# Loading the first two tiles and the input weights in another order, in an eight-core encoder step

## The chip, the cores and the metric

The kernel runs on one Trainium2 chip, on all 8 of its cores, with no traffic between them. Each core has its own engines: TensorE (PE), VectorE (DVE), ScalarE (ACT), GpSimd (POOL), SyncE (SP), and 16 DMA engines that all of a core's transfers share. The metric is the device time of the slowest core in microseconds; lower is better.

## The reference

One layer of an encoder trunk over 16384 prompt tokens and 8 x 32 sample tokens, width 1024. What matters here is its first half:

```
h  = RMSNorm(x)
z  = h @ W_in                      # 2048 columns, [B | C | v | u]
a  = B * causal_dwconv3(C * v)     # 512 channels
b  = scale * blockdiag_linear(trailing_mean(u) - u)   # windows 2, 4, 8, 16
x  = x + concat(a, b) @ W_out
x  = x + relu(RMSNorm(x) @ W_up)^2 @ W_down
x  = x + (p @ W_ple) * sigmoid(RMSNorm(x) @ W_ple_gate)
```

and a final RMSNorm. The last rows of C*v and of u are returned as states.

## The kernel before

Each core takes 2048 prompt tokens and 32 sample tokens, as NT = 5 tiles of 416 columns; x is held transposed, channels on the partitions, as 8 blocks k of 128 channels. Tile 0 has 16 columns of halo more (432). All of x stays in SBUF: X[0] to X[4]. Weights are cast from f32 in DRAM to bf16 by the transfers that POOL issues; x (f32) comes by transfers that SP or ACT issue.

W_in comes in eight pieces, win 0 to win 7 (`loadwin`, L782), each for two groups of 128 columns, in the order of `ZORDER`: u0 u1 | u2 u3 | v0 v1 | c0 c1 | b0 b1 | v2 v3 | c2 c3 | b2 b3. Tile t above 0 comes in two halves of four blocks (`loadx`, L786). The names used below:

- H(t): the tile times its gain in bf16, eight ACT instructions (`Norm.xg`, L472; the first stage does not multiply by 1/rms until PSUM is read).
- `Norm.pre`: squares of x (L493 on DVE, L494 on ACT) and their sum over blocks (L501, L510).
- S(t): the sum over partitions, a matmul with ones in f32 (L564), then the root on ACT (L547) and four reciprocals on DVE (L551), which everything that reads z from PSUM waits for: u (L633), v (L657), c (L662), b (L676).
- For u, POOL or DVE form the trailing sums (L641), DVE the difference (L646). For c, ACT (L665) and DVE (L668) form the convolution, and DVE or POOL scale it (L672).
- PE: z groups L608, block-diagonal matmuls L683, W_out groups L696. The first W_out group waits for everything of tile 0. After it come W_up (L722) and W_down (L734) for most of the time.

PE's program order is the order in which the code is written: the 16 matmuls of u0 and u1 of tile 0 (those of u0 each wait for their own block of H), S(0), then u2 to v1 of tile 0, then u0 to u3 of tile 1, S(1), and then the rest of tile 0 from c0 on. On ACT, DVE and POOL the order comes from a list scheduler (`Prog.schedule`), which simulates the program with assumed costs and a simple model of the transfers, and so gives another order when transfers move. Every engine then runs its list in order: an instruction that waits holds up all behind it. A transfer is issued by its engine in that order too, and `after` names transfers that must have landed first.

Before the change, SP issues blocks 0-1 and 4-5 of tile 0, ACT blocks 2-3 and 6-7. POOL issues win 0 at once; win 1 after blocks 0-1, win 2 after blocks 4-5, and the later ones each two or three transfers on. Tile 1 is issued once win 0 has landed, tile 2 once the first half of W_out has.

Of the kernel before, what the change touches and what calls it, by code (L numbers as in the profile page):

```python
# [12 lines left out]
KD = 8  # L13
# [6 lines left out]
TW0 = TN + NHALO  # L20
# [277 lines left out]
def build_program(debug=False):  # L298
    nc = bass.Bass("TRN2", target_bir_lowering=False)

    def din(name, shape):
        return nc.dram_tensor(name, list(shape), F32, kind="ExternalInput").ap()
# [4 lines left out]
    xt0 = din("xt0", (128, KD * TW0)); xt = din("xt", (NT - 1, 128, KD * TN))  # L307
# [13 lines left out]
    pg = Prog(nc)  # L321
# [4 lines left out]
    def vbf(off, n):  # L326
        return arena[:, off // 4: off // 4 + n // 2].bitcast(BF16)
# [13 lines left out]
    X = []  # L341
# [28 lines left out]
    wout = vbf(wout_o, 8192).rearrange("p (h k n) -> p h k n", h=2, k=KD)  # L370
# [410 lines left out]
    def loadwin(h, after=()):  # L781
        return pg.dma("pool", lambda e: e.dma_start(out=win[:, h, :, :], in_=w_in[h].rearrange("p (k n) -> p k n", k=KD)), 1024,  # L782
                      writes=[("win", h)], after=after)

    def loadx(t, after):
        return [pg.dma("sp", lambda e, hf=hf: e.dma_start(out=X[t][:, 4 * hf:4 * hf + 4, :],  # L786
                                                          in_=xt[t - 1][:, 4 * hf * TN:(4 * hf + 4) * TN].rearrange("p (k n) -> p k n", k=4)),
                       4 * TN / 2.0, writes=[("x", t, 4 * hf + i) for i in range(4)], after=after) for hf in range(2)]

    pg.dma("act", lambda e: e.dma_start(out=cst, in_=cstd), 90, writes=[("cst",)])  # L790
    wq = [loadwin(0)]
    xq = []
    for q4, eng in ((0, "sp"), (1, "act"), (2, "sp"), (3, "act")):
        xq.append(pg.dma(eng, lambda e, q4=q4: e.dma_start(out=X[0][:, 2 * q4:2 * q4 + 2, :],
                                                           in_=xt0[:, 2 * q4 * TW0:(2 * q4 + 2) * TW0].rearrange("p (k n) -> p k n", k=2)),
                         TW0, writes=[("x", 0, 2 * q4), ("x", 0, 2 * q4 + 1)]))
    pg.op("dve", lambda e: e.memset(epsb, EPS), 0.1, writes=[("epsb",)])
    pg.op("dve", lambda e: e.memset(ones, 1.0), 0.1, writes=[("ones",)])
    pg.op("act", lambda e: e.activation(out=RT[3][:, 0:1], in_=epsb[:, 0:1], func=AF.Sqrt), 0.2, reads=[("epsb",)],
          writes=[("rt", 3)], table="sqrt")  # L800
    wq.append(loadwin(1, [xq[0]]))
    wq.append(loadwin(2, [xq[2]]))
    pg.dma("pool", lambda e: e.dma_start(out=wpl, in_=w_pool.rearrange("p (g n) -> p g n", g=4)), 128, writes=[("wpl",)])
    x1 = loadx(1, [wq[0]])
    wq.append(loadwin(3, [wq[1]]))
    wq.append(loadwin(4, [wq[2]]))
    wq.append(loadwin(5, [x1[1]]))
    wq.append(loadwin(6, [wq[4]]))
    wq.append(loadwin(7, [wq[5]]))
    wo = [pg.dma("pool", lambda e, h=h: e.dma_start(out=wout[:, h, :, :], in_=w_out[h].rearrange("p (k n) -> p k n", k=KD)), 2048,  # L810
                 writes=[("wout", h)], after=[wq[6 + h]]) for h in range(2)]
    loadx(4, loadx(3, loadx(2, [wo[0]])))


    pg.op("dve", lambda e: e.tensor_copy(out=CS.hcv[:, :, 0:2], in_=sthist[:, :, 0:2]), 0.1, reads=[("cst",)],
          writes=[("hcv", "s", c) for c in range(4)])
    pg.op("dve", lambda e: e.tensor_copy(out=CS.U[:, :, 0:15], in_=sthist[:, :, 2:17]), 0.1, reads=[("cst",)],
          writes=[("U", "s", c) for c in range(4)])
# [124 lines left out]
    for g in range(3):  # L943
        i = A + 4 * g
# [4 lines left out]
    i = A + 12  # L949
# [120 lines left out]
```

How the kernel before makes its waits and increments, by code:

```python
            def body(h):  # L221
                seen = {}
                for n in self.order[e]:
                    need = {}
                    for m in n.preds:
                        if m.eng == "pe" and e == "pe":
                            continue
                        k = ("d", m.i) if m.dma else m.eng
                        if m.val > need.get(k, (0,))[0]:
                            need[k] = (m.val, m.sem)
                    for k, (val, sem) in need.items():
                        if seen.get(k, 0) < val:
                            seen[k] = val
                            h.wait_ge(sem, val)
                    last = None
                    for f in n.fns:
                        last = f(h)
                    last.then_inc(n.sem, 16 if n.dma else 1)
                if e == "sp":
                    for n in self.nodes:
                        if n.store:
                            h.wait_ge(n.sem, 16)
```

## Time and profile before

| | us |
|---|---|
| median of 3 runs (lowest, highest) | 781.02 (780.72, 781.67) |
| the profiled execution's own time | 780.47 |
| its span (slowest core, core 6) | 778.9 |
| spans of the 8 cores | 775.8 to 778.9 |
| PE busy | 725.7 (93%) |
| DVE busy | 577.5 (74%) |
| ACT busy, POOL busy | 287.4, 225.5 |

The span runs from a core's first to its last instruction; 1.6 us of the execution lie around it. In the rows further down, a row of the timeline gives the start and the length of one group of like instructions in us, counted from the span's start, and in brackets how long the engine had been idle and what ended that. "DMA to landing" is the time from the issue of a transfer until its completion is seen. Where a row of queues stands, q0 holds POOL's transfers, q1 SP's and q10 ACT's: packets, MB written, and their time as a share of the 16 DMA engines in the window.

### The profile page before, as it was taken

The numbers are of one execution on the slowest core, as the hardware profiler recorded it, in microseconds if no ns is written. First come the engines' busy times: TensorE is split into PE (matmuls) and PEld (weight loads), VectorE is DVE, ScalarE is ACT, GpSimd is POOL, SyncE is SP. The second block draws the span as 40 slices with busy tenths as digits, with TensorE's granted clock in tenths as the row PEclk, the third lists the DMA queues.
The fourth block names the chain that finished last, engine by engine and source line by source line (L and its number), as shares of the span: only waits on it lengthen the run. The fifth ranks groups of instructions, "written<-read, shape, count | busy, mean of one in ns | idle before, by whom it ended". The sixth has DMA issues, their size and how long they took to land.

```text
span 778.9 us, 12700 instructions; the slowest of 8 cores (775.8 to 778.9 us)
## 1 busy us (share of the span) xinstructions
PE 725.7 (93%) x3996; PEld 397.1 (51%) x3996; DVE 577.5 (74%) x974; ACT 287.4 (37%) x450; POOL 225.5 (29%) x252
## 2 busy tenths in 40 slices
PE   1889899999899999999999999999999999999862
PEld 0445455555455555555555555555555555555431
DVE  3698989999856765666566557767887886797976
ACT  3425635352562122112211218533333433633442
POOL 1356565757212000000000002034233433334223
PEclk9999999999999999999999999999999999999997
DMA  8877200006609533344323344325466971685212
GB/s 182 171 119 219 89 1 1 1 1 109 111 17 158 95 55 55 64 81 75 55 54 55 57 74 81 72 45 87 86 150 120 156 164 33 113 162 116 53 70 88
DMA packets 13681, 68.04 MB, mean 87 GB/s; under 512 B 1712, under 2 KB 3632, under 8 KB 8368
## 3 DMA queue, kind: packets, MB, share of 16 engines
q0 software_dynamic: 8064, 49.96, 38.0%
q1 hardware_dynamic: 5120, 16.29, 5.8%
q10 hardware_dynamic: 432, 0.98, 0.5%
q8 instruction: 34, 0.56, 0.3%
q14 instruction: 31, 0.25, 0.1%
HBM read 108.59 MB, written 8.59 MB: 150 GB/s over the span
## 4 chain that ended last, share of the span: by engine, by line
PE 83%; DVE 6%; issue 4%; DMA 3%; ACT 2%; POOL 1%; DVEq 0%; SPq 0%; ACTq 0%; POOLq 0%
PE ps L734 28%; PE ps L722 28%; PE ps L608 9%; PE ps L751 7%; PE ps L696 6%; PE ps L744 2%; DMA arena<-xt 2%; DMA arena<-w_in 2%; DVE arena L551 1%; PE ps L564 1%; PE ps L535 1%; DVE arena L668 1%; ACT arena L494 1%; DVE arena L690 1%; ACT arena L472 1%
## 5 line engine op out<-in xcount | busy, mean ns | idle before, releaser
L690 DVE TENSOR_TENSOR arena<-arena,ps 128x416 f32<-128x416 f32 x360 | 206.7, 582 | 39.9 <-PE ps L696 8.9
L734 PE MATMUL ps<-arena 128*128 128x416 bf16 x1280 | 235.7, 339 | 0.0
L722 PE MATMUL ps<-arena 128*128 128x416 bf16 x1280 | 233.4, 341 | 0.0
L722 PEld LDWEIGHTS ps<-arena 128*128 128x128 bf16 x1280 | 125.6, 98 | 102.6 <-issue 4.6
L734 PEld LDWEIGHTS ps<-arena 128*128 128x128 bf16 x1280 | 125.2, 98 | 100.9 <-issue 1.9
L727 ACT ACTIVATE arena<-arena 128x416 bf16<-128x416 f32 x160 | 86.5, 548 | 232.1 <-DVE arena L725 230.3
L725 DVE SCALAR_TENSOR_TENSOR arena<-ps,arena 128x416 f32<-128x416 f32 x160 | 93.7, 586 | 87.1 <-PE ps L722 77.9
L608 PE MATMUL ps<-arena 128*128 128x416 bf16 (+1 forms) x640 | 127.0, 349 | 22.8 <-DMA arena<-w_in 14.6
L608 PEld LDWEIGHTS ps<-arena 128*128 128x128 bf16 x640 | 63.3, 100 | 80.8 <-issue 34.2
L472 ACT ACTIVATE arena<-arena 128x416 bf16<-128x416 f32 (+1 forms) x120 | 71.5, 634 | 34.2 <-DVE arena L690 17.2
L501 POOL TENSOR_TENSOR arena<-arena 128x416 f32<-128x416 f32 (+1 forms) x45 | 65.7, 1462 | 47.2 <-ACT arena L494 29.9
L551 DVE RECIPROCAL arena<-arena 128x104 f32<-128x104 f32 (+3 forms) x75 | 62.9, 839 | 14.0 <-ACT arena L547 13.1
L768 POOL TENSOR_TENSOR arena<-arena 128x416 f32<-128x416 f32 x37 | 41.4, 1125 | 99.2 <-DVE arena L766 75.3
L494 ACT ACTIVATE arena<-arena 128x1664 f32<-128x1664 f32 (+1 forms) x35 | 54.7, 1567 | 32.2 <-PE ps L564 14.5
L751 PE MATMUL ps<-arena 128*128 128x416 bf16 x320 | 62.0, 339 | 2.3 <-ACT arena L472 2.3
L696 PE MATMUL ps<-arena 128*128 128x416 bf16 x320 | 61.6, 339 | 1.3 <-DVE arena L676 1.3
L715 POOL DMA_DIRECT2D arena<-w_down x19 | 10.5, 550 | 148.1 <-PE ps L734 134.6
L641 POOL TENSOR_TENSOR arena<-arena 128x416 f32<-128x416 f32 (+11 forms) x48 | 42.2, 881 | 28.6 <-DVE arena L633 17.3
L712 POOL DMA_DIRECT2D arena<-w_up x19 | 10.5, 554 | 131.3 <-PE ps L722 119.3
L764 ACT ACTIVATE arena<-arena 128x416 f32<-128x416 f32 x40 | 21.7, 549 | 65.2 <-DVE arena L762 65.0
L751 PEld LDWEIGHTS ps<-arena 128*128 128x128 bf16 x320 | 31.3, 98 | 27.7 <-issue 3.0
L696 PEld LDWEIGHTS ps<-arena 128*128 128x128 bf16 x320 | 31.3, 98 | 26.5 <-issue 1.6
(63 smaller groups left out, 433.2 us busy)
## 6 DMA issues: line engine op xcount, KB each, us to landing
arena<-w_up POOLq DMA_DIRECT2D x19, 1024.0 KB, 9.9
arena<-w_down POOLq DMA_DIRECT2D x19, 1024.0 KB, 9.9
yt<-arena SPq DMA_DIRECT2D x20, 416.0 KB, 5.0
arena<-xt SPq DMA_DIRECT2D x8, 832.0 KB, 8.2
arena<-w_in POOLq DMA_DIRECT2D x8, 512.0 KB, 9.8
arena<-w_out POOLq DMA_DIRECT2D x2, 1024.0 KB, 13.1
arena<-w_gate POOLq DMA_DIRECT2D x1, 2048.0 KB, 17.7
arena<-ppt POOLq DMA_DIRECT2D x5, 208.0 KB, 12.8
```

Source lines behind the costliest of these rows:

```text
L472: pg.op("act", lambda e, k=k: e.activation(out=HBUF[i][:, k, 0:n], in_=xs(t, k, self.full), func=AF.Copy, scale=gcol[:, g, k:k + 1]), c_ac ...
L494: return e.activation(out=out, in_=src, func=AF.Square)
L501: pg.op(adders, lambda e, m=m, base=base: e.tensor_tensor(out=SQA[:, base:base + m], in0=SQA[:, base:base + m], in1=SQA[:, base + m:base + ...
L551: pg.op("dve", lambda e, a=a: e.reciprocal(out=rt[:, a:min(a + q, n)], in_=rt[:, a:min(a + q, n)]), 0.06 + 0.0065 * q, reads=[rk], writes= ...
L608: fns = [lambda e, k=k: e.matmul(PS[b][:, 0:zn], lhsT=win[:, ch, k, half * 128:half * 128 + 128], rhs=HBUF[hi][:, k, 0:zn], start=(k == 0) ...
L690: pg.op("dve", lambda e: e.tensor_tensor(out=xs(t, d), in0=xs(t, d), in1=PS[b][:, 0:TN], op=ALU.add), c_dve(TN), reads=[("ps", b), ("x", t ...
L696: pg.op("pe", [lambda e, k=k, ki=ki: e.matmul(PS[b][:, 0:TN], lhsT=wout[:, d // 4, k, (d % 4) * 128:(d % 4) * 128 + 128], rhs=MIX[t % 2][: ...
L722: pg.op("pe", [lambda e, k=k: e.matmul(PS[b][:, 0:TN], lhsT=UPB[j % 2][:, k, c * 128:(c + 1) * 128], rhs=hs(t, k), start=(k == 0), stop=(k ...
L725: pg.op("dve", lambda e: e.scalar_tensor_tensor(out=TMP[rs], in0=PS[b][:, 0:TN], scalar=0.0, in1=RM[t], op0=ALU.max, op1=ALU.mult), c_dve( ...
L727: pg.op("act", lambda e: e.activation(out=FT[w % NFT][:, c, :], in_=TMP[rs], func=AF.Square), c_act(TN), reads=[("tmp", rs)], writes=[("fT ...
L734: pg.op("pe", [lambda e, i=i, j=j, w=w, k=k: e.matmul(PS[b][:, 0:TN], lhsT=DNB[j % 2][:, k, d * 128:(d + 1) * 128], rhs=FT[w % NFT][:, k, ...
L751: pg.op("pe", [lambda e, k=k: e.matmul(PS[bg][:, 0:TN], lhsT=wgate[:, k, d * 128:(d + 1) * 128], rhs=hs(t, k), start=(k == 0), stop=(k == ...
```

## The change

Tile 0 comes in two halves of four blocks (`L793` of the changed kernel), both issued by SP, and tile 1's two halves stand right behind them on SP with nothing to wait for. POOL issues win 0, win 1, win 2 and the pooling weights at once. Win 3 waits for win 0, win 4 for win 1 and so on; the halves of W_out wait for win 5 and win 6 where they waited for win 6 and win 7; tile 2 waits for win 6.

```diff
     wq = [loadwin(0)]
-    xq = []
-    for q4, eng in ((0, "sp"), (1, "act"), (2, "sp"), (3, "act")):
-        xq.append(pg.dma(eng, lambda e, q4=q4: e.dma_start(out=X[0][:, 2 * q4:2 * q4 + 2, :],
...
-                         TW0, writes=[("x", 0, 2 * q4), ("x", 0, 2 * q4 + 1)]))
+    for hf in range(2):
+        pg.dma("sp", lambda e, hf=hf: e.dma_start(out=X[0][:, 4 * hf:4 * hf + 4, :],
...
+               2 * TW0, writes=[("x", 0, 4 * hf + i) for i in range(4)])
+    loadx(1, ())
...
-    wq.append(loadwin(1, [xq[0]]))
-    wq.append(loadwin(2, [xq[2]]))
+    wq += [loadwin(1), loadwin(2)]
     pg.dma("pool", ... w_pool ...)
-    x1 = loadx(1, [wq[0]])
-    wq.append(loadwin(3, [wq[1]]))
-    wq.append(loadwin(4, [wq[2]]))
-    wq.append(loadwin(5, [x1[1]]))
-    wq.append(loadwin(6, [wq[4]]))
-    wq.append(loadwin(7, [wq[5]]))
-    wo = [... after=[wq[6 + h]]) for h in range(2)]
-    loadx(4, loadx(3, loadx(2, [wo[0]])))
+    for h in range(3, 8):
+        wq.append(loadwin(h, [wq[h - 3]]))
+    for h in range(2):
+        ... after=[wq[5 + h]])
+    loadx(4, loadx(3, loadx(2, [wq[6]])))
```

PE's order is the same. The scheduler's lists move. At the head of ACT's list (128x432 is tile 0, 128x416 tile 1):

```order
-L794 DMA arena<-xt 128x864 x2
 L799 ACTIVATE arena<-arena 128x1
-L472 ACTIVATE arena<-arena 128x432 x7
+L472 ACTIVATE arena<-arena 128x432 x6
 L494 ACTIVATE arena<-arena 128x864
-L472 ACTIVATE arena<-arena 128x432
+L472 ACTIVATE arena<-arena 128x432 x2
 L547 ACTIVATE arena<-ps,arena 128x432
-L472 ACTIVATE arena<-arena 128x416 x8
-L494 ACTIVATE arena<-arena 128x1664 x2
+L472 ACTIVATE arena<-arena 128x416 x4
+L494 ACTIVATE arena<-arena 128x1664
```

ACT no longer issues parts of tile 0, and the first square of tile 1 (L494) now stands between the two halves of H(1); the second follows them.

Further on in ACT's list, around the r2 of tile 1 (L572) and the convolutions of c2 and c3 of tile 0 (L665):

```order
 L686 ACTIVATE arena<-ps,arena 128x416 x3
-L572 ACTIVATE arena<-arena 128x416
 L665 ACTIVATE arena<-arena 128x416
 L686 ACTIVATE arena<-ps,arena 128x416
+L572 ACTIVATE arena<-arena 128x416
+L494 ACTIVATE arena<-arena 128x1664
 L665 ACTIVATE arena<-arena 128x416
-L472 ACTIVATE arena<-arena 128x416
+L472 ACTIVATE arena<-arena 128x416 x4
```

The square of tile 2's first half (L494), which waits for that half's transfer, now stands ahead of the convolution of c3; in the kernel before it stood behind it.

DVE, from the sums of tile 1 (L501, L510) to the first group of c (L662):

```order
 L501 TENSOR_TENSOR arena<-arena 128x832
 L501 TENSOR_TENSOR arena<-arena 128x416
+L646 SCALAR_TENSOR_TENSOR arena<-arena 128x416
 L501 TENSOR_TENSOR arena<-arena 128x832
 L657 TENSOR_TENSOR arena<-ps,arena 128x418
 L501 TENSOR_TENSOR arena<-arena 128x416
-L646 SCALAR_TENSOR_TENSOR arena<-arena 128x416
+L657 TENSOR_TENSOR arena<-ps,arena 128x418
 L510 TENSOR_TENSOR arena<-arena 128x416
```

The difference of u1 (L646) moved ahead of the second half of tile 1's sums, and the second v (L657) ahead of the last addition (L510).

## Rows read from the trace of the kernel before

**Rows 1.** Busy time by stretch, slowest core (PE, PEld, DVE, ACT, POOL, granted clock, DMA share, GB/s).
```profile
20.00:40.00 20.00, 17.34 (x82) 8.75 (x81) 12.15 (x19) 9.00 (x13) 7.68 (x13) 1.00 0.81 165
40.00:60.00 20.00, 16.83 (x92) 8.59 (x90) 19.49 (x33) 5.00 (x9) 11.37 (x17) 1.00 0.77 125
```

**Rows 2.** Timeline of PE, slowest core.
```profile
14.57 2.32 PE L608 MATMUL ps<-arena 128*128 128x432 bf16 x6 [14.57 <-DMA arena<-w_in]
...
18.60 3.40 PE L608 MATMUL ps<-arena 128*128 128x432 bf16 x9 [0.84 <-ACT arena L472]
21.80 1.65 PE L564 MATMUL ps<-arena 128*128 128x432 f32 x2
23.24 6.11 PE L608 MATMUL ps<-arena 128*128 128x432 bf16 x32
31.04 5.79 PE L608 MATMUL ps<-arena 128*128 128x416 bf16 x32 [1.70 <-ACT arena L472]
37.79 0.94 PE L564 MATMUL ps<-arena 128*128 128x416 f32 x2 [0.97 <-DVE arena L510]
...
61.90 1.57 PE L696 MATMUL ps<-arena 128*128 128x416 bf16 x8 [1.25 <-DVE arena L676]
```

**Rows 3.** Timeline of ACT, slowest core.
```profile
17.01 0.91 ACT L494 ACTIVATE arena<-arena 128x864 f32<-128x864 f32 x1
...
23.54 0.62 ACT L547 ACTIVATE arena<-ps,arena 128x432 f32<-128x432 f32 x1 [5.08 <-PE ps L564]
...
28.65 2.24 ACT L472 ACTIVATE arena<-arena 128x416 bf16<-128x416 f32 x4 [2.37 <-DMA arena<-xt]
30.80 3.06 ACT L494 ACTIVATE arena<-arena 128x1664 f32<-128x1664 f32 x2
...
55.71 0.64 ACT L665 ACTIVATE arena<-arena 128x416 f32<-128x416 f32 x1 [1.06 <-DVE arena L662]
```

**Rows 4.** Timeline of DVE, slowest core.
```profile
24.26 3.62 DVE L551 RECIPROCAL arena<-arena 128x108 f32<-128x108 f32 x4 [4.21 <-ACT arena L547]
...
30.05 0.58 DVE L646 SCALAR_TENSOR_TENSOR arena<-arena 128x416 bf16<-128x416 f32 x1
...
39.43 1.30 DVE L641 TENSOR_TENSOR arena<-arena 128x428 f32<-128x428 f32 x2 [1.28 <-POOL arena L621]
```

**Rows 5.** Timeline of POOL, slowest core.
```profile
28.75 0.87 POOL L641 TENSOR_TENSOR arena<-arena 128x416 f32<-128x416 f32 x1 [9.99 <-DVE arena L633]
```

**Rows 6.** Transfers by source line: win 0; tile 0's four; tile 1's two; win 6; tile 2's two.
```profile
DMA to landing us min/median/max: 12.8/12.8/12.8
...
DMA to landing us min/median/max: 5.3/9.6/14.4
...
DMA to landing us min/median/max: 9.5/11.7/13.8
...
DMA to landing us min/median/max: 6.0/6.0/6.0
...
DMA to landing us min/median/max: 9.9/10.7/11.5
```

**Rows 7.** DMA queues: windows 6 to 8, 10 to 14, 18 to 26, 20 to 22; whole span.
```profile
q0 software_dynamic: 13, 0.05, 28.7%
...
q0 software_dynamic: 122, 0.43, 66.5%
...
q1 hardware_dynamic: 248, 1.54, 60.2%
q0 software_dynamic: 259, 0.54, 42.0%
...
q1 hardware_dynamic: 60, 0.40, 64.9%
q0 software_dynamic: 61, 0.09, 32.2%
...
q10 hardware_dynamic: 432, 0.98, 0.5%
```

**Rows 8.** Timeline of PE, core 0.
```profile
20.86 0.89 PE L564 MATMUL ps<-arena 128*128 128x432 f32 x2
```

More of the change, by code:

```diff
@@ L791, in build_program @@
     wq = [loadwin(0)]
-    xq = []
-    for q4, eng in ((0, "sp"), (1, "act"), (2, "sp"), (3, "act")):
-        xq.append(pg.dma(eng, lambda e, q4=q4: e.dma_start(out=X[0][:, 2 * q4:2 * q4 + 2, :],
-                                                           in_=xt0[:, 2 * q4 * TW0:(2 * q4 + 2) * TW0].rearrange("p (k n) -> p k n", k=2)),
-                         TW0, writes=[("x", 0, 2 * q4), ("x", 0, 2 * q4 + 1)]))
+    for hf in range(2):
+        pg.dma("sp", lambda e, hf=hf: e.dma_start(out=X[0][:, 4 * hf:4 * hf + 4, :],
+                                                  in_=xt0[:, 4 * hf * TW0:(4 * hf + 4) * TW0].rearrange("p (k n) -> p k n", k=4)),
+               2 * TW0, writes=[("x", 0, 4 * hf + i) for i in range(4)])
+    loadx(1, ())
     pg.op("dve", lambda e: e.memset(epsb, EPS), 0.1, writes=[("epsb",)])
@@ L800, in build_program @@
           writes=[("rt", 3)], table="sqrt")
-    wq.append(loadwin(1, [xq[0]]))
-    wq.append(loadwin(2, [xq[2]]))
+    wq += [loadwin(1), loadwin(2)]
     pg.dma("pool", lambda e: e.dma_start(out=wpl, in_=w_pool.rearrange("p (g n) -> p g n", g=4)), 128, writes=[("wpl",)])
-    x1 = loadx(1, [wq[0]])
-    wq.append(loadwin(3, [wq[1]]))
-    wq.append(loadwin(4, [wq[2]]))
-    wq.append(loadwin(5, [x1[1]]))
-    wq.append(loadwin(6, [wq[4]]))
-    wq.append(loadwin(7, [wq[5]]))
-    wo = [pg.dma("pool", lambda e, h=h: e.dma_start(out=wout[:, h, :, :], in_=w_out[h].rearrange("p (k n) -> p k n", k=KD)), 2048,
-                 writes=[("wout", h)], after=[wq[6 + h]]) for h in range(2)]
-    loadx(4, loadx(3, loadx(2, [wo[0]])))
+    for h in range(3, 8):
+        wq.append(loadwin(h, [wq[h - 3]]))
+    for h in range(2):
+        pg.dma("pool", lambda e, h=h: e.dma_start(out=wout[:, h, :, :], in_=w_out[h].rearrange("p (k n) -> p k n", k=KD)), 2048,
+               writes=[("wout", h)], after=[wq[5 + h]])
+    loadx(4, loadx(3, loadx(2, [wq[6]])))
     pg.op("dve", lambda e: e.tensor_copy(out=CS.hcv[:, :, 0:2], in_=sthist[:, :, 0:2]), 0.1, reads=[("cst",)],
```

## The prediction

> **What bounds the kernel now.** Read first the busy time by stretch, then PE's timeline, then what each wait on it names. PE is busy for 93% of the span, so whatever the loads can give lies in the first 62 us. Three stages are to be seen in PE's timeline. Up to 14.57 PE does nothing: it waits for win 0 [rows 2]. Then it runs u0 and u1 of tile 0, with a wait for the last block of H(0), and S(0) starts at 21.80. Then come 32 matmuls of tile 0, a wait of 1.70 us for H(1), 32 matmuls of tile 1, and S(1) at 37.79, after DVE's last sum [rows 2]. From there to the first W_out group at 61.90 DVE is the bound: it is busy for 19.49 of the 20 us from 40 to 60, PE for 16.83 [rows 1]. After 61.90 PE is nearly gapless, and its order is not touched. So the change is worth what it moves the first W_out group. DVE can't begin this work before S(0), since all that reads z waits for the reciprocals; these start 2.46 us after S(0) (24.26, rows 4). The question is therefore when S(0) comes, and how long DVE takes from it.
>
> I call the start of S(0) s. Before, s = 21.80.
>
> **Win 0 (bounds it).** The 9 matmuls from 18.60 to 21.80 take 0.356 us each, which is 432 columns at 1.2 GHz, while 32 matmuls from 23.24 on take 0.18 [rows 2]; the granted-clock column reads 1.00 in the next stretch [rows 1], so the durations are what tells the level here. 16 of them in a row are 5.7 us, so s is the landing of win 0 + 0.2 + 5.7, if H(0) keeps up. Does win 0 land sooner? It is issued at the same moment. POOL's queue moves its first 13 packets between 6 and 8 [rows 7], so I start it at 7.2. One transfer over 128 partitions is 144 packets (three make ACT's 432, rows 7). Packets of two busy queues alternate: 248 against 259 in 8 us, 60 against 61 in 2 [rows 7]. One of x takes 0.602 x 8 x 16 / 248 = 0.31 us of a DMA engine, one of a weight piece 0.665 x 4 x 16 / 122 = 0.35, so a pair takes 0.66 and 16 engines do 24.3 pairs per us. Win 0 then ends at 7.2 + 144 / 24.3 = 13.1. Before, with 13 packets by 8 and 122 in the 4 us from 10 to 14, I get 13.0, and it landed at 1.55 + 12.8 = 14.35 [rows 6], so the slowest engine adds 1.3. The same tail gives 14.4 now: no change, because one queue of x with long rows replaces two with short ones. Bounds: at the rate of the row from 10 to 14 (0.43 MB in 4 us) 0.524 MB take 4.9 us, landing by 12.1 without the tail; at the rate of the 2 us window (0.09 MB in 2 us) 11.6 us, landing at 18.8, or 20.1 with it. I take 14.4, since the packet count is nearest to this case.
>
> **Tile 0 (hidden now).** Before, its last quarter landed 14.4 us after issue, at 16.4 [rows 6], and ACT's H blocks 6 and 7 with a square (0.91, rows 3) between them let PE's last 9 matmuls start at 18.60. Now SP's queue is alone until 7.2: 144 packets at 16 / 0.31 = 52 per us end by about 6, 65 more by 7.2, the other 79 at 24.3 by 10.5, landing by 11.8. Then 2 copies, the square and 2 copies (0.6, 0.6, 0.9, 0.6, 0.6) give the last block at 15.1; PE wants it at 14.6 + 7 x 0.356 = 17.1. Covered by 2 us. So s = 14.4 + 0.2 + 5.7 = 20.3: **1.5 us earlier**.
>
> **Win 1, win 2, tile 1 (hidden).** Win 1 ends at 13.1 + 5.9 + 1.3 = 20.3, wanted at s + 1.44 = 21.7. Tile 1's 288 packets end at 10.5 + 11.9 = 22.4, landed by 23.7. Win 2 then has 63 of its packets left, at 16 / 0.35 = 46 per us: 23.8, landed at 24.5 to 25.1, wanted at 24.6. A lag of 0.5 there costs nothing, as v1 is done by 28 and H(1) comes later. Win 3 lands near 29, wanted at 36.
>
> **Order of ACT and DVE.** ACT: L547 at s + 1.74, then 4 copies (2.2, rows 3), the square (half of 3.06) and 4 copies (2.2): H(1) at s + 8.2 = 28.5, where it was 30.9. Tile 1's half landed 13.8 us after its issue at 14.79 [rows 6]; this stall goes, and what is late next is ACT itself. DVE: reciprocals, four L633 and L646 end at s + 8.8 (30.63 before, rows 4). The two sums take 1.7; the second L646 waits for POOL, whose first L641 starts at s + 6.95 [rows 5] and whose third ends at s + 11.1 (L641 0.9, L651 0.4, L653 behind DVE's L646, L641 0.9, L621 0.2, L641 0.9). Then, at about 0.5 to 0.6 for 416 columns [rows 4] and double for two blocks, L646 0.6, L501 1.1, L657 0.5, L501 0.5, L657 0.5, L510 0.6: s + 14.9. So S(1) is at s + 15.0, where it was at s + 16.0: **1.0 more**. The block of 34 instructions of DVE from 39.43 [rows 4] to the L676 that lets PE start at 61.90 [rows 2] took 22.2. Its counterpart has one L657 and one L672 more and one L641 less (+0.6) and starts when POOL's next L641 ends, with two weight issues (0.6 each) between: s + 15.7 = 36.0. It ends at 58.8. So the first W_out group moves from 61.90 to about 59.1: **2.8 in all**. Bounds of the order's part (1.3 of it): nothing, if POOL's waits return, and 1.3 more, if DVE's wait of 1.28 for POOL [rows 4] goes too.
>
> **Later transfers.** POOL issues win 6 at about s + 11.1 = 31.4; win 4 and win 5 are before it; it lands in 6.0 or a little more, at 38. Tile 2 is issued then and lands in 9.9 [rows 6], near 48, where it was 68.8. The issue of W_out's halves may hold POOL under 1 us each, hidden in its idle time of 20 - 11.37 [rows 1]. DMA is not busier in sum.
>
> The profiled execution took 780.47 with a span of 778.9; less 2.8 is 777.7. The median of the runs lies 0.55 higher: **778.2**.
>
> **Rivals.**
> 1. *Win 0 late: slower.* Win 0 shares with a queue of x that never runs dry and whose packets are 6.7 KB (0.40 MB in 60). If its rate falls to the 0.09 MB in 2 us of the window from 20 to 22, it lands at 18.8 to 20.1, s is 24.7 to 26.0, and the order's 1.3 don't pay for it: 782.6 to 783.9, say 783.2. It decides from a landing at 17.2 (no gain) and 18.8 (slower by 0.2%). For it: that row. Against: half of those packets were the small ones of the pooling weights, and the count was one for one.
> 2. *Tile 0 no earlier: same.* If its second half lands at 16.4 again, PE waits for H(0) as before, s = 21.8 and only the order's 1.3 are left: 779.7. For it: the same 1.77 MB, now behind one turn in two instead of two in three. The Trainium skill (DMA: Bandwidth & Descriptors, SWDGE vs HWDGE vs iDMA, "Issuing engines are not separate DMA queues") says that issuing from several engines saves only the time of issuing, so that putting the halves on one queue would change nothing by itself. Against: the packets have double length now.
> 3. *Tile 2 late: same.* ACT's square of tile 2 stands ahead of c3's convolution, which was at 55.71 [rows 3] and would be at 52.9; with 1.5 for the square, tile 2 must have landed by 51.4. I get 48; with the 13.8 of tile 1's second half [rows 6] 51.8, costing 0.4; at 54.2 the whole gain is gone, 780.5.
> 4. *Short packets: same.* A queue cuts long rows to 4 KB: tile 1 then needs 416 turns and lands near 30.5, H(1) at 32.7, S(1) near 38: 781. The rows speak against it, 0.40 MB in 60 packets [rows 7]. The Trainium skill (same page and section) calls packets of at most 4096 B the preferred size; the trace here has larger ones.
> 5. *The clock rises sooner: faster.* On core 0 the two matmuls of S(0) took 0.89 us [rows 8], against 1.65 here: 2.4 GHz before them. PE had been in matmuls with two gaps. Without these gaps the rise may fall into u1: 0.7 from S(0) and about 1.2 from six or seven matmuls, s + 1.44 some 1.9 sooner: 776.3.
>
> **How the numbers follow.** Forecast 0.45 (777.0 to 779.2), rival 1 0.14, rival 2 0.16, rival 3 0.08, rival 4 0.02, rival 5 0.15. A measurement of this kernel tells from no change about 0.2%, 1.56 us. Faster: forecast and rival 5, 0.60. Same: rivals 2 to 4 and 0.02 of rival 1, 0.28. Slower: 0.12. The range of 775.8 to 781.8 leaves out rival 1 and the far end of rival 5.
>
> **What would show it.** Right: win 0 landing within 14 to 15, PE starting then and running 16 matmuls without a gap, S(0) near 20.3, H(1) by 28.6, S(1) at 15 us behind S(0), the first W_out group near 59. Wrong: a gap in the 16 matmuls (rival 2), win 0 landing after 17 (rival 1), ACT waiting for tile 2 before c3 (rival 3), or a W_out group at 59 with a span that is not shorter; then a later wait, of the kind that DVE's reciprocals give PE at the start of each tile, would have eaten it.

## The result, and the profile after

The changed kernel takes 782.12 us (median of 22 runs), the kernel before 781.03 in the same comparison (22 runs): a ratio of 1.0015, with 95% in 1.0009 to 1.0021. It is 1.1 us slower; 778.2 was forecast.

| | before | after |
|---|---|---|
| the profiled execution's own time | 780.47 | 782.24 |
| its span, and the spans of the 8 cores | 778.9 (775.8 to 778.9) | 780.3 (776.2 to 780.3) |
| PE busy, DVE busy | 725.7, 577.5 | 727.1, 577.5 |

In some of the experiments' comparisons one die ran slower in every kernel, the one before too; those numbers are read from the cores of the other die alone.

PE on the slowest core of the changed kernel (columns as in [rows 2]):

```profile
15.93 5.92 PE L608 MATMUL ps<-arena 128*128 128x432 bf16 x16 [15.93 <-DMA arena<-w_in]
21.64 0.95 PE L564 MATMUL ps<-arena 128*128 128x432 f32 x2
22.43 3.08 PE L608 MATMUL ps<-arena 128*128 128x432 bf16 x16
26.70 8.71 PE L608 MATMUL ps<-arena 128*128 128x432 bf16 x48 [1.19 <-DMA arena<-w_in]
37.75 0.94 PE L564 MATMUL ps<-arena 128*128 128x416 f32 x2 [2.35 <-DVE arena L510]
...
63.92 2.93 PE L696 MATMUL ps<-arena 128*128 128x416 bf16 x8 [3.94 <-DVE arena L624]
66.65 2.98 PE L608 MATMUL ps<-arena 128*128 128x416 bf16 x8
69.42 1.64 PE L696 MATMUL ps<-arena 128*128 128x416 bf16 x8
```

The start of the program went roughly as it should. The 16 matmuls have no gap any more, the norm's matmuls take 0.95 where they took 1.65 [rows 2], and a new wait of 1.19 for win 2 stands ahead of v0 of tile 0. What is wrong comes later: the first W_out group, due at 59, starts at 63.92 after a wait of 3.94, and it and the next group take 2.9 each, where [rows 2] has 1.57.

One core's start varies by 2 us, so from here I also use the mean of the eight cores. "u2" is the first wait of PE for DVE's L633 of tile 2, behind S(2). Behind it PE's longer waits are alike before and after (0.92 near 172 us, 2.1 to 2.2 near 209, 2.29, 4.43 and about 3 in the last 50 us); what differs there is the clock, behind u2 itself and behind the wait near 209; the last section tells of it.

| mean of 8 cores, us | PE begins | S(0) | S(1) | first W_out | its wait | its 8 matmuls | S(2) | u2 (wait) |
|---|---|---|---|---|---|---|---|---|
| before | 14.03 | 21.42 | 37.57 | 61.70 | 1.23 | 1.57 | 87.02 | 97.51 (2.45) |
| after | 15.22 | 20.20 | 36.74 | 62.54 | 4.15 | 2.74 | 89.82 | 98.50 (1.49) |

S(0) is 1.2 earlier, S(1) 0.8, the first W_out group 0.8 later, S(2) 2.8 later, and of that 1.8 comes back until u2. 1.0 is left. From u2 to the end the mean core takes 679.5 where it took 680.2; the slowest core's span is 1.4 longer, the median of the runs 1.1.

Who holds W_out back? First ACT on core 4, whose W_out group waits 5.19:

```profile
50.90 0.56 ACT L572 ACTIVATE arena<-arena 128x416 f32<-128x416 f32 x1
53.76 1.59 ACT L494 ACTIVATE arena<-arena 128x1664 f32<-128x1664 f32 x1 [2.29 <-DMA arena<-xt]
55.25 0.63 ACT L665 ACTIVATE arena<-arena 128x416 f32<-128x416 f32 x1
```

ACT stands before the square of tile 2's first half (L494) until its transfer has landed; only then comes the convolution of tile 0's c3 (L665, [rows 3] has it at 55.71 with no square ahead). On six of eight cores this wait is there, 0.42 to 2.29 us. On the other two, core 3 among them, ACT reaches the square when tile 2 has just landed. POOL and DVE of core 3:

```profile
56.11 3.40 POOL L501 TENSOR_TENSOR arena<-arena 128x832 f32<-128x832 f32 x2 [2.60 <-ACT arena L494]
61.16 1.06 POOL L672 TENSOR_TENSOR arena<-arena 128x416 f32<-128x416 f32 x1 [1.65 <-DVE arena L668]
```
```profile
56.18 1.91 DVE L624 COPY arena<-arena 128x2 f32<-128x2 f32 x1
58.01 0.58 DVE L672 TENSOR_TENSOR arena<-arena 128x416 f32<-128x416 f32 x1
58.51 1.45 DVE L668 SCALAR_TENSOR_TENSOR arena<-arena 128x416 f32<-128x416 f32 x1
...
63.10 0.57 DVE L676 TENSOR_TENSOR arena<-ps,arena 128x416 bf16<-128x416 f32 x1
```

POOL waits for that square too: its next two instructions are sums of tile 2 (L501, 3.40 us), and c3's scaling (L672) stands behind them, at 61.16. From its start to the W_out group it is 2.76 us on every core. And while POOL adds, a copy of two columns takes DVE 1.91 us, where a like copy just before took 0.16, and L668 takes 1.45 for 0.64. So here it is not the sums themselves that end last: on all eight cores POOL is idle again for 0.59 to 1.66 us behind them, until DVE's last L668 of c3 is done. From the convolution to the scaling it is 4.15 to 5.34 us (4.52 on the mean); before it was 3.42.

How late was tile 2? The answers for its issues on core 4, the only ones of L786 between 36 and 45:

```profile
L786 SPq DMA_DIRECT2D arena<-xt x2: 328/914/1500, 39.0 to 39.4; - x2
DMA to landing us min/median/max: 14.6/18.2/21.8
```

Issued at 39.0, landed near 53.7. In [rows 6] its halves took 9.9 and 11.5. The stretches that answer to [rows 1], core 3:

```profile
20.00:40.00 20.00, 16.47 (x79) 8.26 (x77) 13.72 (x19) 8.91 (x13) 11.52 (x20) 0.97 0.95 168
40.00:60.00 20.00, 18.97 (x96) 9.47 (x94) 17.64 (x30) 8.62 (x14) 9.92 (x12) 0.94 1.02 206
```

From 40 to 60 the DMA engines move 206 GB/s where they moved 125, and DVE, the bound of this stretch before with 19.49 busy, now has 2.36 us of waits in it.

### The profile page after: what moved, and what is told of

It reads as the page before. It is cut to its first block, busy times and chain, and to the rows that moved or that the text cites. A ratio compares the mean times of both kernels' runs of the same rounds, so it can differ in the third digit from the quotient of the medians.

```text
span 780.3 us, 12689 instructions; the slowest of 8 cores (776.2 to 780.3 us)
## 1 busy us (share of the span) xinstructions
PE 727.1 (93%) x3996; PEld 398.2 (51%) x3996; DVE 577.5 (74%) x974; ACT 288.4 (37%) x450; POOL 225.9 (29%) x252
## 4 chain that ended last, share of the span: by engine, by line
PE 84%; DVE 6%; issue 5%; DMA 2%; ACT 2%; POOL 1%; DVEq 0%; ACTq 0%; POOLq 0%
PE ps L734 28%; PE ps L722 28%; PE ps L608 10%; PE ps L751 7%; PE ps L696 7%; PE ps L744 2%; DMA arena<-w_in 2%; DVE arena L551 2%; PE ps L564 1%; PE ps L535 1%; DVE arena L668 1%; POOL arena L501 0%; ACT arena L665 0%; DVE arena L584 0%; ACT arena L472 0%
## 5 line engine op out<-in xcount | busy, mean ns | idle before, releaser
L690 DVE TENSOR_TENSOR arena<-arena,ps 128x416 f32<-128x416 f32 x360 | 207.8, 583 | 42.1 <-PE ps L696 11.5
L472 ACT ACTIVATE arena<-arena 128x416 bf16<-128x416 f32 (+1 forms) x120 | 72.0, 636 | 31.1 <-DVE arena L690 16.7
L501 POOL TENSOR_TENSOR arena<-arena 128x416 f32<-128x416 f32 (+1 forms) x45 | 65.1, 1447 | 46.4 <-ACT arena L494 30.2
L696 PE MATMUL ps<-arena 128*128 128x416 bf16 x320 | 63.1, 344 | 3.9 <-DVE arena L624 3.9
L494 ACT ACTIVATE arena<-arena 128x1664 f32<-128x1664 f32 (+1 forms) x35 | 54.9, 1570 | 31.6 <-PE ps L564 13.9
L696 PEld LDWEIGHTS ps<-arena 128*128 128x128 bf16 x320 | 31.6, 99 | 30.1 <-issue 5.9
L751 PEld LDWEIGHTS ps<-arena 128*128 128x128 bf16 x320 | 31.4, 98 | 27.8 <-issue 3.3
```

The costliest lines, as they stand in the source:

```text
L472: pg.op("act", lambda e, k=k: e.activation(out=HBUF[i][:, k, 0:n], in_=xs(t, k, self.full), func=AF.Copy, scale=gcol[:, g, k:k + 1]), c_ac ...
L494: return e.activation(out=out, in_=src, func=AF.Square)
L501: pg.op(adders, lambda e, m=m, base=base: e.tensor_tensor(out=SQA[:, base:base + m], in0=SQA[:, base:base + m], in1=SQA[:, base + m:base + ...
L690: pg.op("dve", lambda e: e.tensor_tensor(out=xs(t, d), in0=xs(t, d), in1=PS[b][:, 0:TN], op=ALU.add), c_dve(TN), reads=[("ps", b), ("x", t ...
L696: pg.op("pe", [lambda e, k=k, ki=ki: e.matmul(PS[b][:, 0:TN], lhsT=wout[:, d // 4, k, (d % 4) * 128:(d % 4) * 128 + 128], rhs=MIX[t % 2][: ...
L751: pg.op("pe", [lambda e, k=k: e.matmul(PS[bg][:, 0:TN], lhsT=wgate[:, k, d * 128:(d + 1) * 128], rhs=hs(t, k), start=(k == 0), stop=(k == ...
```

## The experiments

I call the list scheduler the planner. Theory A: the transfers are worth something, and the planner's lists of ACT, DVE and POOL, made for a tile 2 that lands early, lose more. Theory B: the transfers themselves cost the time (win 0, win 2, the load on the queues). In the kernels of e5, e6, e9, e10 and e13 line numbers are higher by 4, in e4 and e11 only those behind the added matmuls (L696 is the filling there, L700 the W_out group). For e1 to e4 the number is the span of the slowest of cores 0 to 3 (before: 786.1), for e13 and e14 that of cores 4 to 7 (before: 778.9), medians of 8 to 11 runs.

**e1, e7 and e14: tell the planner that tile 2 is late.** All transfers are those of the changed kernel.

```diff
-                end = wire + 2.0
+                end = max(wire + 2.0, n.told)
...
-    loadx(4, loadx(3, loadx(2, [wq[6]])))
+    x2 = loadx(2, [wq[6]]); x2[0].told, x2[1].told = (68.0, 71.0); loadx(4, loadx(3, x2))
```

> The changed kernel with every transfer as it is; only the scheduler is told that tile 2 lands at 68 and 71 us, so that the lists of ACT, POOL and DVE put the squares and sums of tile 2 (L494, L501) behind the convolutions of c2 and c3. Theory A (the order costs it: tile 2's sums on POOL lengthen the end of tile 0 on DVE, PE then waits 4 us and runs its next 24 or so matmuls at 1.2 GHz): the wait before the first W_out group falls from 3.9 to under 2 us, that group takes 1.57 us and not 2.9, and the time is 780.0 (779.3 to 780.8). Theory B (the transfers cost it: PE starts 1.2 us later and win 2 lands late): nothing changes, 782.1.

e1 took 782.5 on cores 0 to 3, 3.6 below before, with W_out at 60.55 (before 61.88) and 8 matmuls in 1.57. The same kernel on another chip, all cores:

> The kernel of e1 once more, on another chip. There, on cores 0 to 3, the first W_out group started at 60.6 (62.6 in the changed kernel, 61.9 before) and the second tile's next u groups at 94.1 (98.8 and 97.7). Theory A: 777.8 (777.0 to 779.5). If what is won by 94 us is lost again later, on the waits near the end or in the clock: 780 to 781.

e7 took **775.39** us (6 runs) against 781.19: ratio 0.9913, 0.9888 to 0.9938. That is 6.7 us below the changed kernel (about 8 by the two ratios, as that one was measured on another chip), by the order of the lists alone: tile 2's first half still lands at 53.5 on the mean, 53.6 in the changed kernel. PE on its slowest core:

```profile
61.35 1.57 PE L696 MATMUL ps<-arena 128*128 128x416 bf16 x8 [0.40 <-DVE arena L676]
```

**e2 and e8: tile 2 issued later.** The changed kernel with tile 2 behind the first half of W_out, as before the change.

```diff
-    loadx(4, loadx(3, loadx(2, [wq[6]])))
+    loadx(4, loadx(3, loadx(2, [wo[0]])))
```

> The changed kernel with tile 2 issued behind the first half of W_out, as in the kernel before; scheduler and transfers then agree. Theory A: as e1, 780.0 (779.3 to 780.8), with the first W_out group at about 60.5 on the average core. Theory B: 782.1. A third one (W_out's first half is what PE waits for at 63.9): the wait gets shorter as W_out has the DMA engines alone, but the order makes no difference between e1 and e2: e1 782.1, e2 below 781.

e2: 785.6 on cores 0 to 3 (-0.5, less than the runs scatter), W_out at 59.87. On another chip, all cores:

> The kernel of e2 once more, on another chip: there the second tile's u groups started at 95.1 on cores 0 to 3, 2.5 us sooner than before. Theory A: 778.6 (777.6 to 780). If it is lost again later: 780 to 781.

e8: 778.13 us (9 runs), ratio 0.9952 (0.9933 to 0.9971), W_out at 59.86. This is the time that was forecast for the changed kernel.

**e3: only tile 2 early.** The kernel before, with tile 2 issued behind win 6.

```diff
-    loadx(4, loadx(3, loadx(2, [wo[0]])))
+    loadx(4, loadx(3, loadx(2, [wq[6]])))
```

> The kernel before with one part of the change alone: tile 2 is issued behind win 6. Theory A: the squares and sums of tile 2 again come ahead of the end of tile 0, the first W_out group waits about 4 us and starts at 1.2 GHz: 782.5 (781.8 to 784). Theory B: no change, 781.0.

787.65 on cores 0 to 3 (+1.55), W_out at 65.96 (+4.1). The expected wait of 4 us at 1.2 GHz did not come: PE waits 1.95 before the group, which takes 1.57; the rest of the lateness lies ahead of it. ACT on core 3:

```profile
51.57 1.59 ACT L494 ACTIVATE arena<-arena 128x1664 f32<-128x1664 f32 x1 [7.34 <-DMA arena<-xt]
```

A loss comes with this one line of the change alone.

**e5 and e6: lists and transfers crossed.** The order of each engine's list is forced to that of the other kernel.

```diff
-                    if n.eng is not None:
+                    if n.eng is not None or (nxt and not n.dma and nxt[e] is not n):
```

> The transfers of the changed kernel, with the lists of ACT, DVE and POOL (all but the transfers in them) exactly as in the kernel before. Theory A (the lists cost it): the wait before the first W_out group is under 2 us, that group starts near 60.5, and the time is 779.5 (778.5 to 780.5). POOL's list has the two halves of W_out early, so it may stand still for win 5 and win 6, which could take 1 us of it back. Theory B (the transfers cost it): 782.

e5, new transfers and old lists: 781.48 (12 runs), ratio 0.9995 (0.9981 to 1.0009), 2 us over what theory A expected. W_out at 61.48, u2 at 97.33: only 0.2 ahead of before, although S(0) is 1.0 and S(1) 1.9 ahead. Where the lead goes is seen on DVE. From S(1) to the W_out group its wait for POOL ahead of L645 is 2.27 on the mean, where it was 0.96, and its waits for PE are 0.35 longer (core 1):

```profile
39.14 1.30 DVE L645 TENSOR_TENSOR arena<-arena 128x428 f32<-128x428 f32 x2 [2.04 <-POOL arena L625]
```

> The transfers of the kernel before, with the lists of the changed one. Tile 2 lands at about 69 here, and the square that waits for it stands ahead of the convolution of c3. Theory A: that holds ACT until 69, the first W_out group starts after 75, 10 us and more late, and the time is 790 (786 to 796). Theory B: as the kernel before, 781.

e6, old transfers and new lists: 790.27 (6 runs), ratio 1.0105 (1.0081 to 1.0128), the 790 of theory A. ACT and PE on core 7:

```profile
64.02 1.59 ACT L498 ACTIVATE arena<-arena 128x1664 f32<-128x1664 f32 x1 [6.96 <-DMA arena<-xt]
```
```profile
72.42 2.93 PE L700 MATMUL ps<-arena 128*128 128x416 bf16 x8 [10.17 <-DVE arena L628]
```

The new transfers cost nothing with the old lists (and bring nothing), and the new lists lose the more the later tile 2 lands. Theory B is out.

**e4 and e11: fill the wait.** The changed kernel with 16 matmuls without use ahead of the first W_out group, to see whether the fall of the clock is the loss.

```diff
+        if (t, d) == (0, 0):
+            pg.op("pe", [lambda e, i=i: e.matmul(PS[b][:, 0:TN], lhsT=win[:, 0, i % 8, 0:128], rhs=HBUF[HA[1]][:, i % 8, 0:TN],
...
```

> The changed kernel with 16 matmuls more on PE, of 416 columns, ahead of the first W_out group and into its PSUM bank, where nothing reads them: they need only what PE already has. The lists of the other engines are the same. They take 2.8 us of the wait of 4 us. Theory A with the clock: the W_out group starts at the same time but takes 1.57 us and not 2.9, S(2) comes 2.5 us sooner, and of that about half is left at the next wait for the reciprocals: 780.9 (780.2 to 781.5). If the clock were no part of it: 782.1, or more where the new matmuls delay anything.

e4: 786.05 on cores 0 to 3, level with the kernel before; the changed kernel was not run beside it.

> The kernel of e4 once more (16 matmuls that nothing reads fill PE's wait before the first W_out group), on another chip. There, on cores 0 to 3, the W_out group started at the same time but took 1.57 us, and the next tile's u groups came at 97.1 instead of 98.8. If the clock costs the changed kernel that much: 780.6 (780 to 781.2). If not: 782.1.

e11: 782.82 (12 runs), ratio 1.0020 (1.0007 to 1.0033), no gain over the changed kernel's 1.0015. PE on its slowest core:

```profile
57.58 2.98 PE L696 MATMUL ps<-arena 128*128 128x416 bf16 x16
64.95 2.93 PE L700 MATMUL ps<-arena 128*128 128x416 bf16 x8 [4.40 <-ACT arena L472]
```

The 16 matmuls run at once, and the wait behind them is still 4.40 here: a poor test of the clock on this core. On the mean the wait was 1.99 and the group 2.00, and S(2) came only 0.6 earlier than in the changed kernel. That the fall of the clock costs up to 1.4 us per group of 8 is seen in the rows; that the time is shorter without it, this experiment didn't show. Core by core it shows more: on cores 1, 4 and 6 the group starts at 61.0 to 61.7 after a wait of 1.0 to 1.2, takes 1.57, and S(2) comes 25.3 behind it. Cores 1 and 2 of the changed kernel start it at 61.3 and 61.8, it takes 2.8 and 2.9, and S(2) comes 27.0 and 27.7 behind it. That puts the clock at about 2 us there; but the slowest core decides the time, and on that one the wait stayed.

**e9, e10 and e13: move single positions of the lists.** The changed kernel, with POOL's two sums of tile 2 behind c3's scaling (e9), with ACT's square of tile 2 behind c3's convolution (e10), with both (e13).

```diff
+        pg.lists["pool"] = [n for n in pool[:k + 1] if n not in early] + early + pool[k + 1:]
...
+        act[k], act[k + 1] = act[k + 1], act[k]
```

> The changed kernel with one move in one list: POOL's first two sums of tile 2 (L501 of 832 and 416 columns, 3.4 us together, from 56.1 in its trace) stand behind the scaling of c3 (L672) and not ahead of it. Transfers and all other lists as in the changed kernel. Theory A1 (POOL's sums do it: while they run, DVE's small copy L624 takes 1.9 us and a tap L668 1.4, and L672 comes late): the first W_out group starts 1.9 us sooner (60.6 on the average core, 62.5 in the changed kernel), with no wait above 2.5 us, at 2.4 GHz: 779.3 (778 to 780.5). Theory A2 (ACT's square of tile 2 ahead of c3's convolution does it): 782.

e9: 782.41 (12 runs), ratio 1.0018 (1.0002 to 1.0033), W_out at 62.73. No gain over the changed kernel's ratio. ACT on core 4:

```profile
56.35 1.59 ACT L498 ACTIVATE arena<-arena 128x1664 f32<-128x1664 f32 x1 [3.31 <-DMA arena<-xt]
57.85 0.63 ACT L669 ACTIVATE arena<-arena 128x416 f32<-128x416 f32 x1
```

From the convolution to POOL's scaling it is 2.6 us now, where it was 4.15 to 5.34, but the convolution still waits for tile 2: that lands 2.1 us later in this execution, on the mean, than in the changed kernel's, and the squares begin as much later. On core 1 alone ACT did not wait, and there the W_out group starts at 60.98 after 1.52.

> The changed kernel with one move in ACT's list: the square of tile 2's first half stands behind the convolution of c3 (L665). Theory A2: that convolution comes 1.5 us sooner, and the first W_out group 1.5 us, PE's wait falls to 2.6 us, the clock stays up: 779.5. Theory A1: POOL's sums only start up to 0.7 us later, DVE's end of tile 0 is as long: 781.5 to 782.3.

e10: 783.56 (12 runs), ratio 1.0037 (1.0025 to 1.0049), W_out at 62.25. No gain. ACT and POOL on core 0:

```profile
54.55 0.64 ACT L669 ACTIVATE arena<-arena 128x416 f32<-128x416 f32 x1 [0.56 <-DVE arena L666]
56.34 1.59 ACT L498 ACTIVATE arena<-arena 128x1664 f32<-128x1664 f32 x1 [1.14 <-DMA arena<-xt]
```
```profile
58.07 3.31 POOL L505 TENSOR_TENSOR arena<-arena 128x832 f32<-128x832 f32 x2 [5.05 <-ACT arena L498]
61.35 1.05 POOL L676 TENSOR_TENSOR arena<-arena 128x416 f32<-128x416 f32 x1
```

The convolution is free of tile 2, but POOL still does its two sums before the scaling. Each of the two moves leaves the other link in place. Hence e13.

> The changed kernel with both moves of the lists at once: on ACT the square of tile 2's first half stands behind the convolution of c3, on POOL the first two sums of tile 2 stand behind the scaling of c3; all else as in the changed kernel. The traces of the two single moves show two links in one chain: with POOL alone moved, ACT still waits for tile 2 (to 53.9 to 56.6 on the eight cores) before c3's convolution; with ACT alone moved, POOL's two sums (3.3 to 3.7 us) still stand ahead of c3's scaling, and that scaling comes 2.9 to 4.0 us behind the start of that wait's end in either. Theory A (the two links in series, each alone enough to hold c3 back): with both gone c3 waits for nothing of tile 2. In the core of the ACT move where the convolution was at 54.6 DVE's part was done at 57.0, so POOL's scaling is at about 57.1 and the first W_out group at about 60.0 (57.1 + 2.8), with a wait of 1.0 to 1.5 and 8 matmuls in 1.57 on nearly all cores. The time is near that of the kernels whose planner put both later: between 775.4 and 778.1, I say 777.5, ratio 0.993 to 0.997. Theory B (a single list position is not it, the whole of the lists must be planned anew, with DVE's waits for POOL moving elsewhere): first W_out group still near 62, time 781 to 783.

e13: W_out at 59.80 (forecast 60.0), wait 1.52, all eight cores at 1.57. On core 4:

```profile
59.96 1.57 PE L700 MATMUL ps<-arena 128*128 128x416 bf16 x8 [1.51 <-DVE arena L680]
...
92.75 1.57 PE L612 MATMUL ps<-arena 128*128 128x416 bf16 x8 [1.86 <-DVE arena L680]
96.94 1.42 PE L612 MATMUL ps<-arena 128*128 128x416 bf16 x6 [2.45 <-DVE arena L637]
```

But the slowest of cores 4 to 7 took 778.45 (median of 8 runs), before 778.9 (11 runs): 0.45 less, which is within the scatter of the runs, where 3 to 4 were expected. Theory A is right on the place, and wrong on the price. W_out is 1.9 earlier than before, u2 only 0.9. PE's wait of 1.86 was 0.71 before. POOL's sums now stand one step further on, ahead of u3's trailing sum, and DVE waits for that one on all eight cores:

```profile
58.22 3.50 POOL L505 TENSOR_TENSOR arena<-arena 128x832 f32<-128x832 f32 x2
61.67 0.90 POOL L645 TENSOR_TENSOR arena<-arena 128x430 f32<-128x430 f32 x1
```
```profile
62.68 0.59 DVE L645 TENSOR_TENSOR arena<-arena 128x416 f32<-128x416 f32 x1 [2.14 <-POOL arena L645]
```

> The same kernel as the one whose planner is only told that tile 2 lands at 68 and 71 us, on the same chip as the run beside it, so that the two can be compared with each other. If its 775.39 of the other chip is not a thing of that chip: ratio to the kernel before 0.989 to 0.994, first W_out group at about 60.1, the 8 matmuls in 1.57 on all cores, and the stretch from the wait near 207 us to the last norm (near 660) at 2.4 GHz on all cores. Theory A expects the kernel with both moves 1 to 3 us above it at most; theory B 5 us or more.

e14, on the same chip: 773.1 on cores 4 to 7, 5.8 below before and 5.35 below e13. DVE reaches the reciprocals of tile 2 at 86.79 on core 4, e13 at 92.52:

```profile
86.79 0.79 DVE L551 RECIPROCAL arena<-arena 128x104 f32<-128x104 f32 x1
87.51 0.52 DVE L676 TENSOR_TENSOR arena<-ps,arena 128x416 bf16<-128x416 f32 x1
```
```profile
92.52 3.51 DVE L555 RECIPROCAL arena<-arena 128x104 f32<-128x104 f32 x4
```

In the lists of e7 and e14 the reciprocals of tile 2 stand one by one between what tile 1 still needs. In e13 all four stand in one block behind it, and so they do before the change, in the changed kernel and in e8; before, on core 4:

```profile
94.34 3.50 DVE L551 RECIPROCAL arena<-arena 128x104 f32<-128x104 f32 x4
```

From the first W_out group to the first of them DVE takes 31.4 us before, 31.5 after, 31.1 in e8, 32.4 in e13 and 27.6 in e7 (means of 8 cores). So c3's order is the cause of the late W_out group. What e7 has over e13 does not show at W_out or at S(2), where the two are within 0.4 us, but behind S(2): 2.9 us at u2, with the earlier reciprocals.

The kernels side by side, as in the table above:

| mean of 8 cores, us | PE begins | S(0) | S(1) | first W_out | its wait | S(2) | u2 (wait) |
|---|---|---|---|---|---|---|---|
| e5, old lists | 15.34 | 20.39 | 35.68 | 61.48 | 1.06 | 86.80 | 97.33 (2.45) |
| e7, told late | 15.45 | 20.68 | 37.03 | 60.14 | 1.10 | 85.45 | 93.68 (1.03) |
| e8, tile 2 late | 15.22 | 20.34 | 36.61 | 59.86 | 1.02 | 85.18 | 95.36 (2.32) |
| e13, both moves | 15.44 | 20.55 | 36.93 | 59.80 | 1.52 | 85.73 | 96.58 (2.33) |

**e12: tile 0 in quarters again.** e7's kernel with tile 0's four quarters on SP and ACT.

```diff
-    for hf in range(2):
-        pg.dma("sp", ...
+    for q4, eng in ((0, "sp"), (1, "act"), (2, "sp"), (3, "act")):
+        xq.append(pg.dma(eng, ...
```

> The kernel of e1 with tile 0 in four quarters on SP and ACT as before; tile 1 without a wait, the weights two ahead, and the scheduler told of tile 2 stay. If the two halves matter (H(0) not waited for, 16 matmuls of u0 and u1 without a gap): S(0) is at 21.5 or later instead of 20.7, and the time is 0.8 above e1's 775.4 on the same chip: 776.2 to 777. If only tile 1 and the weights count: 775.4, within 0.4.

780.95 (12 runs), ratio 1.0005 (0.9995 to 1.0014); e7 was not run on this chip, its ratio was 0.9913. S(0) is at 24.60 on the mean. ACT on core 5:

```profile
19.61 0.92 ACT L494 ACTIVATE arena<-arena 128x864 f32<-128x864 f32 x1 [4.45 <-DMA arena<-xt]
```

The last quarter, on ACT's queue beside tile 1 on SP's and three weight pieces on POOL's, lands 17.5 us after its issue, where it took 14.4 with tile 1 held back [rows 6]. With tile 1 issued at once, the halves in front of it on one queue are what keeps tile 0 early: 3.9 us at S(0), of which 2.9 are left at the first W_out group (63.04). I had expected 776.2 to 777. The lists were planned anew here too, so not all of the loss in time is shown to be the transfers'.

## Why the prediction was wrong

The stages, each by its own step:

- **"Win 0: no change."** It landed 14.1 us after its issue on the slowest core, at 15.6 for 14.4, 12.8 before [rows 6]; PE begins 1.2 later on the mean. Rival 1 had the direction; its price needed a landing at 17.2.
- **"Tile 0 (hidden now)": right.** The halves landed 6.9 and 12.6 after issue, the second at 14.1 for 11.8; the 16 matmuls still have no gap. **"s: 1.5 us earlier": nearly right**, 1.2 on the mean (20.20 for 20.3). Here two misses cancel, which is luck: PE begins at 15.2 for 14.6, and the stretch to S(0) takes 5.0 for 5.7, since rival 5's clock rise came with it (0.95 for the two matmuls of the norm).
- **"Win 2 … costs nothing."** It landed 23.8 after its issue at 2.8, at 26.6 for 24.5 to 25.1; PE waits 1.19 (core 3). As forecast it is not on the path: H(1) was done at s + 7.4 (forecast s + 8.2), and DVE's sums come last.
- **"Order of ACT and DVE: 1.0 more."** This failed first. S(1) came 16.5 behind S(0) on the mean, not 15.0; before it was 16.15. The term took POOL's durations as they stood. They grew: of POOL's rows

```profile
29.99 0.81 POOL L653 TENSOR_TENSOR arena<-arena 128x16 bf16<-128x16 f32 x1 [0.86 <-DVE arena L646]
...
31.60 0.56 POOL L621 COPY arena<-arena 128x15 f32<-128x15 f32 x1
...
39.52 0.22 POOL L653 TENSOR_TENSOR arena<-arena 128x16 bf16<-128x16 f32 x1
```

the first stands beside DVE's sums and the last does not. DVE waits for them:

```profile
33.10 0.59 DVE L646 SCALAR_TENSOR_TENSOR arena<-arena 128x416 bf16<-128x416 f32 x1 [0.99 <-POOL arena L641]
...
36.67 0.93 DVE L510 TENSOR_TENSOR arena<-arena 128x416 f32<-128x416 f32 x1
```

- **"First W_out group about 59.1, 2.8 in all."** The step that decides, and it failed by 3.4: 62.54. In e7, with the same transfers, it is 60.14, so 1.0 of the 3.4 comes from the stages ahead. Of the rest 1.3 is c3's convolution, at 55.27 on the mean behind tile 2's square and 53.95 in e7, and 1.1 is the way from there to the scaling, 4.52 for 3.42. The counterpart of the block of 34 DVE instructions was counted, but not what stands beside it on ACT and POOL. The part "Later transfers" let tile 2 land near 48, from the 9.9 of [rows 6], which had been measured with the first half of W_out already landed. Now both halves, 1 MB each, are under way with it, and it took 14.6; in e3, where it is issued ahead of both, 7.3 on the mean of the eight cores.
- **Rival 3 (0.08) was the mechanism.** It has the whole gain gone at a landing of 54.2 (at 781.0 by its own sum, not the 780.5 that it names). Tile 2's first half landed at 53.6 on the mean, so 0.6 of the 2.8 should have been left at the W_out group; 0.8 was lost instead. Its price was too low, since it saw ACT alone. POOL's two sums of tile 2 behind the square (3.3 to 3.7) and DVE's slower work beside them come on top, and so does the level of the clock: 4.15 us of wait, then 2.74 instead of 1.57 for 8 matmuls, with S(2) 27.3 behind W_out where it was 25.3.

With tile 2 issued behind the first half of W_out as before and the lists that go with it (e8), the forecast's chain holds within 0.8 us: W_out at 59.86 for 59.1, and 778.13 us. Tile 2 lands at 59.3 there, on the mean, where it was 66.2 before. With only c3's order mended (e13), W_out is at 59.80 and the time that of before within the scatter: here the last sentence of the forecast came true, "a W_out group at 59 with a span that is not shorter". What stays open is which positions of the lists behind c3 make the rest of e7's gain. The reciprocals of tile 2 are the visible difference, but no single position there was tried.

## What to carry to other kernels

A list scheduler plans with modelled landings. A transfer that is issued earlier is not only a load on the queues: it pulls its consumers ahead in every in-order list, and if it lands late, all that stands behind them is late, also work that has nothing to do with it. After moving a transfer, look in each engine's list at what now stands directly behind its first reader, on every engine of the chain: two links can each hold the same result, and then mending one shows nothing in the time. The cheapest test is to leave the transfers alone and tell the planner a late landing.

## What the runs showed of the hardware

The clock of TensorE falls from 2.4 to 1.2 GHz after some waits, core by core: the group behind a W_out group starts 2.73 us behind it after the change (63.92 to 66.65 above), 0.34 us for each matmul of 416 columns, and 1.41 us before the change on core 0, 0.18 for each. The wait for L633 behind S(2) is 2.45 us on every core before, and on four of eight the 16 matmuls behind it take 4.52 to 4.66 us:

```profile
97.72 4.66 PE L608 MATMUL ps<-arena 128*128 128x416 bf16 x16 [2.45 <-DVE arena L633]
```

On the other four they take 2.97. After the change this wait is 1.49 and no core loses; in e7 it is 1.0, and none loses. The wait of 2.1 to 2.2 at 204 to 212 us (L683) is in all of these kernels. From it to the next S it takes either 28.3 to 28.9 or 29.9 to 30.0 us: the long one on five cores before, on all eight after, on four in e5 and e8, on none in e7 and e14's cores 4 to 7. On core 4, before and after (columns as in [rows 1]):

```profile
200.00:250.00 50.00, 47.89 (x275) 26.64 (x274) 34.15 (x66) 28.69 (x50) 12.27 (x14) 1.00 0.62 105
```
```profile
200.00:250.00 50.00, 47.84 (x265) 26.19 (x264) 33.30 (x66) 28.32 (x48) 12.30 (x14) 0.97 0.54 93
```

275 matmuls at a granted clock of 1.00, 265 at 0.97. For e7 this is the second part of the gain: 3.8 at u2, and up to 1.7 at each of the two waits on cores that lost it before. Why the same wait costs in one kernel on all cores and in another on none, the runs don't tell.

And operations of one vector engine grow beside those of the other: in the changed kernel a DVE copy of two columns takes 0.16 us, and 1.91 while POOL adds 832 columns (core 3); an L668 of 416 columns takes 0.64, and 1.90 beside the same adds (core 4).
